# Modulation units of a first mixer moved into the feed-forwards behind it, and that mixer's border in the common form

## What is computed

```python
mod = (c_act @ ada_w[i] + ada_b[i]).reshape(B, N_SUB, 3, D_MODEL)

def swiglu(h, w1, w3, w2):
    return (jax.nn.silu(h @ w1) * (h @ w3)) @ w2

def sublayer(x, fn, g_pre, g_post, shift, scale, gate, weight):
    hmod = rms_norm(x, g_pre) * (1 + scale[:, None, :]) + shift[:, None, :]
    y = rms_norm(fn(hmod), g_post)
    return x + weight * gate[:, None, :] * y
```

## Time and profile before

| | us |
|---|---|
| median of three runs | 1425.66 (1424.58 to 1426.38) |
| span of the profiled execution | 1421.9 |
| PE busy | 1394.5 |
| PE weight loads busy | 1185.4 |
| DVE busy | 1024.9 |
| ACT busy | 719.7 |
| GpSimd busy | 90.4 |

### The profile page before, as it was taken

One profiled execution on the slowest core, in us unless ns is written; L12 is line 12 of the kernel. 1 busy time (PEld: TensorE's weight loads), 2 busy tenths in 40 slices (PEclk: granted clock), 3 DMA queues, 4 the chain that ended last, 5 costly groups with the idle time before them and its releaser, 6 DMA issues.

```text
span 1421.9 us, 18024 instructions
## 1 busy us (share of the span) xinstructions
PE 1394.5 (98%) x7310; PEld 1185.4 (83%) x7310; DVE 1024.9 (72%) x1296; ACT 719.7 (51%) x931; POOL 90.4 (6%) x118
## 2 busy tenths in 40 slices
PE   9999999998999999999999999999999999999997
PEld 8788888977888878888789978788888889998886
DVE  5887677987987668777767976678745654664865
ACT  5543356456444455343565676554334644555433
POOL 1000001001000010000000352100000100000000
PEclk9999999999999999999999999999999999999999
DMA  9898865855988848888535522478755454445542
GB/s 385 339 351 303 319 247 198 320 193 201 391 308 298 325 162 324 318 311 332 200 135 186 209 74 89 178 299 336 283 206 207 178 204 167 148 170 186 199 149 111
DMA packets 50498, 339.07 MB, mean 238 GB/s; under 512 B 6720, under 2 KB 8432, under 8 KB 10352
## 3 DMA queue, kind: packets, MB, share of 16 engines
q1 hardware_dynamic: 50416, 337.92, 63.8%
HBM read 336.81 MB, written 2.66 MB: 239 GB/s over the span
## 4 chain that ended last, share of the span: by engine, by line
PE 78%; DVE 12%; ACT 4%; DMA 2%; issue 2%; POOL 1%; SPq 0%; ACTq 0%; DVEq 0%; POOLq 0%
PE ps L1045 76%; DVE wlo L1704 4%; DMA raw<-units 2%; DVE hf L2126 2%; DVE M L1714 1%; ACT whi L558 1%; PE ps L1263 1%; PE ps L1154 1%; ACT hf L639 0%; POOL base L474 0%; POOL ssx L475 0%; DVE xboth L1779 0%; DVE wlo L1709 0%; PE ps L1528 0%; DVE xboth L2061 0%
## 5 line engine op out<-in xcount | busy, mean ns | idle before, releaser
L1045 PE MATMUL ps<-whi,xboth 128*128 128x512 f32 x2864 | 912.2, 393 | 6.5 <-DVE wlo L1709 1.7
L1045 PEld LDWEIGHTS ps<-whi,xboth 128*128 128x128 f32 x2864 | 538.3, 188 | 125.4 <-issue 4.7
L1704 DVE TENSOR_TENSOR wlo<-raw,whi 128x2048 fp32r<-128x2048 f32 x212 | 486.2, 2298 | 178.5 <-ACT whi L558 178.0
L1045 PE MATMUL ps<-wlo,xboth 128*128 128x512 f32 x1432 | 558.5, 390 | 0.0
L558 ACT ACTIVATE whi<-raw 128x2048 fp32r<-128x2048 f32 x218 | 416.9, 1915 | 170.8 <-DMA raw<-units 170.7
L1045 PEld LDWEIGHTS ps<-wlo,xboth 128*128 128x128 f32 x1432 | 269.5, 188 | 52.6
L1045 PE MATMUL ps<-xboth,whi 128*128 128x256 f32 (+1 forms) x1152 | 254.6, 310 | 0.1
L1045 PEld LDWEIGHTS ps<-xboth,whi 128*128 128x128 f32 x1152 | 187.9, 190 | 12.4 <-ACT hf L829 0.3
L1045 PE MATMUL ps<-xboth,wlo 128*128 128x256 f32 x704 | 198.1, 281 | 0.0
L1714 DVE SCALAR_TENSOR_TENSOR M<-M 128x1024 f32<-128x1024 f32 x160 | 189.3, 1220 | 0.1
L1045 PEld LDWEIGHTS ps<-xboth,wlo 128*128 128x128 f32 x704 | 133.9, 190 | 0.0
(11 more groups left out here) (242 smaller groups left out, 881.2 us busy)
## 6 DMA issues: line engine op xcount, KB each, us to landing
raw<-units SPq DMA_DIRECT2D x218, 1024.0 KB, 4.9
M<-ada_units SPq DMA_DIRECT2D x82, 1024.0 KB, 7.1
M<-units SPq DMA_DIRECT2D x10, 1024.0 KB, 5.3
gp<-gate_rows SPq DMA_DIRECT2D x7, 512.0 KB, 6.1
bias_copies<-bias_by_distance SPq DMA_DIRECT2D x1, 1536.0 KB, 9.6
M<-cvec SPq DMA_DIRECT2D x2, 512.0 KB, 4.4
x<-x_in SPq DMA_DIRECT2D x1, 1024.0 KB, 6.0
ada_a<-ada_units SPq DMA_DIRECT2D x1, 1024.0 KB, 20.0
```

The source lines that it names most:

```text
L1045: return pe.matmul(out, lhsT, rhs, start=start, stop=stop, skip_group_check=True)
L1704: dve.tensor_tensor(rest(u), landed(u), rounded(u).bitcast(F32), ALU.subtract).then_inc(w_lo, 1)
```

## The change

It has two parts that belong together.

The modulation units: `ADA_FIRST` of stage 2 becomes 32 and of stage 3 52, so that the first mixer has six of them (26 to 31), and stages 2 and 3 have 20 each instead of 18. `ada_in_block` gives two to each block and three to blocks 4 and 6 of these two stages. `gate_columns(2)` moves to block 4 of stage 2. In the mixer's tail on DVE the four units `v + 6` to `v + 9` are gone, `mod_columns(2)` stands where one of them stood, and `heads_out(1)` moves ahead of a remainder.

The border: stage 2 joins `outside` and `landing`, the late form is dropped, and in the mixer ACT rounds the units 16, 17 and 18 (the next stage's 0, 1 and 2) ahead of `boundary`, and DVE does the remainder of unit 16. SP loads the next stage's unit 1 at the mixer's end, ahead of its unit 0, and in stage 2 it waits for `w_lo` and `w_used` before the first two modulation loads as it does in stage 3.

```diff
-ADA_FIRST = {0: 8, 1: 26, 2: 36, 3: 54, 5: 72}
-ADA_BLOCKS = {0: 9, 2: 9, 3: 9, 5: 6}
+ADA_FIRST = {0: 8, 1: 26, 2: 32, 3: 52, 5: 72}
+ADA_LAST = {0: 25, 1: 31, 2: 51, 3: 71, 5: 83}
+def ada_in_block(n, i):
+    if i > {0: 9, 2: 9, 3: 9, 5: 6}[n]:
+        return 0
+    return 3 if n in (2, 3) and i in (4, 6) else 2
...
-        outside = {FIRST[n] + 1: n for n in (1, 3, 4, 5, 6)}
-        landing = {FIRST[n] + 3: n for n in (1, 3, 4, 5, 6)}
+        outside = {FIRST[n] + 1: n for n in range(1, 7)}
+        landing = {FIRST[n] + 3: n for n in range(1, 7)}
...
-                    if n == 3:
+                    if n in (2, 3):
                         sp.wait_ge(w_lo, u0 + 4)
                     load_ada(v)
                     load(down_unit(n, 0))
-                    if n in (3, 5):
+                    if n in (2, 3, 5):
                         sp.wait_ge(w_used, u0 + 2)
...
-                        for _ in range({6: 1, 7: 1, 8: 0, 9: 0, 10: 2, 15: 2}.get(u, u > 10)):
+                        for _ in range({6: 1, 7: 1, 10: 2, 11: 1, 12: 1}.get(u, 0)):
                             load_ada(v)
                             v += 1
...
+                    load(FIRST[n + 1] + 1)
```

ACT, mixer and border:

```diff
                     hi(u0 + 15)
                     turned_hi(1)
-                    hi(u0 + 16)
-                    boundary(n, True)
+                    for u in range(16, 19):
+                        hi(u0 + u)
+                    boundary(n)
...
                 square_y(n, 0)
                 square_x(n + 1, 0)
-                hi(u + 1 if late else u + 3)
+                hi(u + 3)
                 modulated(n + 1, 0, 0)
                 modulated(n + 1, 0, 1)
-                square_y(n, 1, (0,))
-                if late:
-                    hi(u + 2)
-                square_y(n, 1, (1,))
-                if late:
-                    hi(u + 3)
+                square_y(n, 1)
```

DVE, mixer and border:

```diff
                     denominator(2)
                     denominator(3)
-                    ada(v + 6)
                     after_piece(5, u0 + 8)
                     turned_lo(0, (0, 1))
-                    ada(v + 7)
+                    ada_done(v + 5)
+                    mod_columns(n + 1)
+                    heads_out(1)
                     after_piece(7, u0 + 8)
-                    heads_out(1)
                     turned_lo(1, (0,))
                     lo(u0 + 15)
                     turned_lo(1, (1,))
-                    ada(v + 8)
-                    boundary(n, True)
+                    lo(u0 + 16)
+                    boundary(n)
...
-                if not late:
-                    lo(u + 1)
-                    lo_part(u + 2, 0)
+                lo(u + 1)
+                lo_part(u + 2, 0)
                 gated_y(n, 0)
                 new_x(n, 0)
-                if late:
-                    ada(ADA_FIRST[n] + 9)
-                    ada_done(ADA_FIRST[n] + 9)
-                    mod_columns(n + 1)
-                else:
-                    lo_part(u + 2, 1)
-                    lo_part(u + 2, 2)
+                lo_part(u + 2, 1)
+                lo_part(u + 2, 2)
                 normed_x(n + 1, 0)
```

More of the change, by code:

```diff
@@ L281, in load @@
                     else:
-                        sp.wait_ge(a_used[u in outside], (ADA_FIRST[n - 1] + 2 * ADA_BLOCKS[n - 1] - 2 - EARLY) // 2 + 1)
+                        sp.wait_ge(a_used[u in outside], (ADA_LAST[n - 1] - EARLY) // 2 + 1)
                 elif u in held_by:
@@ L364, in _ @@
                     for i in range(3, NF):
-                        some = i < 2 + ADA_BLOCKS[n]
+                        some = ada_in_block(n, i - 1)
                         load(up_unit(n, i, 0))
@@ L370, in _ @@
                         load(down_unit(n, i - 2))
-                        if some:
-                            load_ada(v + 1)
-                            v += 2
+                        for k in range(1, some):
+                            load_ada(v + k)
+                        v += some
                         if i == 7:
@@ L647, in silu_c, with boundary @@
                 act.activation(cb, cb, ACT.Silu).then_inc(S["c_ok"], 1)
-            def boundary(n, late):
+            def boundary(n):
                 u = FIRST[n + 1]
@@ L739, in _ @@
                     hi(u0 + 35)
-                    boundary(n, False)
+                    boundary(n)
                 if kind == "ml":
@@ L1809, in new_x, with boundary @@
                                              in1=x[:, t, v_], op0=ALU.mult, op1=ALU.add).then_inc(x_new[t], 1)
-            def boundary(n, late):
+            def boundary(n):
                 u = FIRST[n + 1]
-                if not late:
-                    lo(u + 1)
-                    lo_part(u + 2, 0)
+                lo(u + 1)
+                lo_part(u + 2, 0)
                 gated_y(n, 0)
                 new_x(n, 0)
-                if late:
-                    ada(ADA_FIRST[n] + 9)
-                    ada_done(ADA_FIRST[n] + 9)
-                    mod_columns(n + 1)
-                else:
-                    lo_part(u + 2, 1)
-                    lo_part(u + 2, 2)
-                normed_x(n + 1, 0)
[L1827 to L1831, removed]
+                lo_part(u + 2, 1)
+                lo_part(u + 2, 2)
+                normed_x(n + 1, 0)
+                lo_part(u + 2, 3)
                 split_first(n + 1, 0)
@@ L1835, in boundary @@
                 modulated(n + 1, 3)
[L1836 to L1840, removed]
+                for q in range(1, 4):
+                    split_x(n + 1, 0, q)
                 gated_y(n, 1)
[L1842 to L1845, removed]
+                lo_part(u + 3, 0)
                 new_x(n, 1)
-                for part in range(0 if late else 1, 4):
+                for part in range(1, 4):
                     lo_part(u + 3, part)
@@ L1937, in _ @@
                         a = up_unit(n, i, 0)
-                        some = i < 1 + ADA_BLOCKS[n]
+                        some = ada_in_block(n, i)
                         lo(a + 3)
@@ L1949, in _ @@
                         lo(a + 5)
[L1950 to L1953, removed]
+                        for k in range(1, some):
+                            ada(v + k)
+                        v += some
+                        if n in (0, 2) and i == 4:
                             ada_done(v - 1)
-                            gate_columns(0)
+                            gate_columns(n)
                         if n == 0 and i == 5:
```

## The result

The changed kernel takes 1429.42 us, median of 8 runs (1427.30 to 1430.79), beside 1425.53 (8 runs) for the kernel before: a ratio of 1.0022, with a 95% interval of 1.0011 to 1.0032. It is slower by 3.9 us. A later comparison gave nearly the same: 1428.44 against 1425.06, 1.0022 (1.0010 to 1.0034). The forecast was 1431.2, the range 1428.0 to 1434.5, slower with a chance of 0.82.

The account below looks back on a forecast made before the run. PE, busy 98% of the span, bounds the kernel. Old border idle -3.74, common border +0.03, tail -0.70, stall +8.2, clock +1.7 give +5.5 us: span 1427.4, plus 3.8 to the median, 1431.2 us; range 1428.0 to 1434.5.

Parts of the forecast that it names:

- The mechanism: Border behind the mixer: f+2 lands late, ACT's squares wait behind its rounding, PE's transposes start at 331.0, 8.2 us late.
- the lower bound of 7.3: Smallest forecast PE wait for the transposes behind the mixer: shortest landing, 4.9 us, and none of the extra 0.6.
- The upper bound for GpSimd: Border behind the mixer: PE's wait could reach 10.0 us if GpSimd's first step took 2.08 us; 0.30 was assumed.
- The waits removed: Three PE waits in the old border, 3.54 us together, and one of 0.70 in the mixer's tail would go.
- the stall: PE's wait for the transposes in the border behind the mixer: 8.2 us, between 7.3 and 10.0.
- the first rival: The border behaves as the common one elsewhere, no stall: -4.1 us, 1421.6 us; chance 0.08.
- The clock: PE's granted clock falls behind the wait in the mixer's border: +1.7 us, between 0 and 3.4.
- The second rival: The stall comes without a clock loss: +2.8 to +3.8 us, 1428.5 to 1429.5; chance 0.17.
- The third units: A third modulation unit in two blocks of each of the next two feed-forwards: no cost, upper bound 9.2 us.
- The term "nothing": Cost set for the third modulation units in four feed-forward blocks: zero, with 3.4 us a block free on DVE.
- The sign that PE stays busy all through the feed-forwards: Expected in the profile after; a feed-forward block with PE waiting for `wlo` or `g` would count as wrong.

Follow-up runs that it names:

- the repeated profile: The changed kernel itself, run and profiled again on the same chip as two other runs: 1428.44 us, against 1425.06 for the kernel before.
- squares_first: Changed kernel; behind the mixer alone ACT rounds f+2 after the squares of tokens 0, and DVE does its remainders after the new x: 1420.51 us, ratio 0.9972.
- early_release: Changed kernel; PE uses the mixer's first output unit for tokens 1 right behind the second unit's tokens 0, freeing its ring place earlier: 1421.19 us, ratio 0.9973.
- before_blocked: Kernel before; behind the mixer ACT rounds the next stage's second unit ahead of the border instead of behind the squares: 1433.38 us, ratio 1.0053.
- units_only: Kernel before with only the changed kernel's modulation units and the earlier heads_out; the border keeps the late form: 1424.11 us, ratio 1.0001.
- the fill: Changed kernel with dummy matmuls on PE just ahead of the transposes of tokens 0 behind the mixer: 1429.11 us with 26, 1427.53 with 32.
- clock_kept: Changed kernel with 26 dummy matmuls on PE just ahead of the transposes of tokens 0 behind the mixer: 1429.11 us, ratio 1.0028.

## Why the prediction was right, and where it was off

**The mechanism** was as forecast at each link. SP's issue: 316.2 forecast, 315.67 measured. Landing 5.2, measured 4.8. ACT waits with its squares behind `hi(u0 + 18)`; first square to transposes 7.66 forecast (7.06 and 0.6), 7.39 measured, which is 0.33 more than in the common border and not 0.6. PE ready at 322.8, measured 322.4. The transposes started at 329.76 and not at 331.0, PE was ready 0.4 earlier, and the wait is 7.32 (7.48 in the repeated profile) where 8.2 was forecast: a few tenths at each link, and it ended at the lower bound of 7.3. `squares_first`, `early_release` and `before_blocked` show that the cause is the order, and not the common form: the first two end the wait, the third makes it in the old form.

**The upper bound for GpSimd**, 10.0, did not come. Its first step took 0.30 us, at 324.68, as taken; DVE had ended `gated_y` at 324.38 and stood idle until 325.74. So the rule of the Trainium skill, GPSIMD Engine Reference, Specifications, on contention with VectorE is not tested by that step.

**The waits removed**: 3.54 + 0.70 forecast gone, and gone. The expectation that the common form saves what the earlier trace rows promise is right, too: without the stall (`squares_first`) it is -3.8 us in the medians, where the first rival had -4.1.

**The clock**: +1.7 forecast (0 to 3.4), 1.9 to 2.4 by the marks, 0.9 by the medians of the times and 1.3 by those of the spans; the forecast lies between and can't be told better. The second rival, a stall without the clock, gave 1428.5 to 1429.5, which holds the measured median; but its mechanism is refuted by the rows, the clock did fall and the fall had its price. That the time agrees with it is the sum of other terms. By the Trainium skill, TensorE: Matmul & The Clock Gate, an idle engine falls to half rate and comes back only after sustained work; the trace now agrees, with half the clock for 10 us around a wait of 7.3.

**The sum over the border.** In the marks, +4.2 (and +4.7 in the repeated profile). The terms that have a row: stall 7.32 (7.48), waits -4.24, clock 1.9 (2.4), together +5.0 (+5.6); so 0.8 to 1.0 us more was gained there than the single waits say. It is not laid to one place.

**The third units.** The term "nothing" was right for the blocks in which they are done. The sign that PE stays busy all through the feed-forwards failed in stage 2, by 0.59 and 0.55 - 0.30 us at its end, and the stage was 1.2 us longer in the profiled pair. But `before_blocked` shows the same without third units. So no cost of them is shown, neither by this nor by the median of `units_only`; stage 3, which has them as well, took 189.1 in both.

**Where the size was off.** The forecast adds +5.5 us to the median of 1425.66; the medians moved by 3.9 and 3.4. The forecast mis-sized the stall, 8.2 where 7.32 came, and 0.8 to 1.0 us of gain had no term. Over the border this makes +4.2 out of +5.5. That the profiled pair lies 5.7 us apart, so close to 5.5, is luck, for it holds 1.2 us of stage 2 and 0.3 of the rest for which the forecast had no term. The pair also exaggerates: each execution of a kernel without the fill took 1.7 to 1.9 us more than its span, so the profiled execution of the kernel before took about 1423.7 (worked out from its span of 1421.9; its own time was not taken), some 2 us under its medians of 1425.53 and 1425.66, while that of the changed kernel, 1429.37, was at its median. The 3.8 us between span and median in the forecast were thus 1.8 of overhead and 2.0 of luck in the one execution that was profiled. Adding the forecast change to the median, as was done, allows for that, but a change read off two profiles doesn't. If the 1.2 us of stage 2 are part of that luck, the +4.2 of the border agrees with the medians; this is argued and not shown.

## What to carry to other kernels

When a border gets weights earlier, ask which of them lands in a place that is released last, and keep its rounding behind the small steps of the chain that PE waits for: in a queue that is worked off in order, one landing of 4.8 us ahead of a square cost a wait of 7.3 us, and 8 us of the program when only that was moved. The idle stretch of PE cost its length and here some 2 us more for the clock. And before laying a difference between two profiles to the change, see how far each profiled execution lies from its median, and look whether a run without the change shows the same.

## What the runs showed of the hardware

The spread between executions of one kernel goes to a good part with TensorE's clock, and in the two profiles with a low mean clock and no stall in the border (`squares_first` at 0.995, `units_only` at 0.993) the clock was low in the second mixer. Of 58 runs of the kernel before, 11 had a mean granted clock of 0.993 to 0.995, with a median of 1428.6 us, and 47 had 0.997 to 0.999, with 1424.3. The stretches 820 to 830 and 870 to 880 of `squares_first`, profiled in its longest execution (1425.24 us):

```profile
820.00:830.00 10.00, 9.52 (x47) 7.91 (x47) 3.79 (x3) 5.71 (x13) 0.99 (x1) 0.66 0.26 91
...
870.00:880.00 10.00, 10.00 (x41) 8.59 (x41) 5.92 (x12) 6.76 (x14) 1.06 (x3) 0.73 0.00 0
```

The kernel before had 0.83 and 1.00 in the same two stretches, `units_only` 0.72 and 0.66. The program is the same in all 58 runs; what lets the clock fall in one and not in another was not tried. So two profiles can differ by 4 us with no change in the kernel. Marks ahead of that mixer leave this part out, but stage 2 shows that they too can hold 1 us that is not the change's.

The fill shows a second thing: 26 matmuls, which took 5.97 us of a wait of 7.5 and left 1.53, held the clock in the border of the profiled execution, but half of the runs had the low mean clock; with 32 (7.31 us, 0.18 left) 10 of 12 runs were at 0.997 or above, and with none, none was. Whether the remaining 1.5 us or chance in the second mixer made the difference wasn't told apart.

The clock also fell where no single wait was long. In `early_release` a wait of 1.98 us was followed by 3.4 us at half the clock. In the kernel before it was at half from about 824.5 to 828, though no wait of PE in the ten us ahead was over 0.68; around a wait of 1.69 in its border, and around the 1.53 of `clock_kept`, it stayed at 1.00. So the length of one wait didn't decide it; what did was not tried.

GpSimd's small step took longer beside a remainder on DVE, and ended 0.17 us after it in both of these rows: the 2.08 us of the earlier trace rows ended at 333.96, the remainder beside it at 333.79; in the changed kernel a step of 0.44 us ended at 328.52, the remainder at 328.35. Alone, the step took 0.30.
